# The opening of a two-layer hybrid encoder: forget-gate products in column groups, token blocks turned while the rows of x arrive

## The reference

```python
proj = x @ w_in                       # 1024 x (3*1024 + 16)
q, k, v, fg = jnp.split(proj, [D_MODEL, 2 * D_MODEL, 3 * D_MODEL], axis=-1)
log_f = jax.nn.log_sigmoid((fg + b_f).astype(jnp.float32))
c = jnp.cumsum(log_f, axis=1).transpose(0, 2, 1)
...
logits = jnp.einsum("bhqd,bhkd->bhqk", q_i, k).astype(jnp.float32) * scale
logits = logits + c_i[..., None] - c[:, :, None, :]
mask = pos_k[None, :] <= pos_q[:, None]
probs = jax.nn.softmax(jnp.where(mask, logits, -jnp.inf), axis=-1)
...
x = layer_norm(ALPHA * x + m, ln1_g[i], ln1_b[i])
```

## Time and profile before

| what | us |
|---|---|
| median of 3 runs | 1293.03 |
| lowest and highest | 1290.93, 1293.05 |
| the profiled execution's own time | 1291.16 |
| its span | 1289.4 |
| PE busy | 1262.9 (98%) |
| POOL busy | 862.1 (67%) |
| DVE busy | 538.6 (42%) |
| ACT busy | 408.1 (32%) |

### The profile page before, as it was taken

The page is one execution under the profiler, slowest core; times in us unless marked ns, Lnnn a source line. Parts: engine busy times, 40 slices in busy tenths (PEclk is TensorE's granted clock), DMA queues, the critical chain, the costliest instruction groups (busy, mean ns, idle before and its releaser), DMA issues.

```text
span 1289.4 us, 17594 instructions
## 1 busy us (share of the span) xinstructions
PE 1262.9 (98%) x5758; PEld 1014.5 (79%) x5758; DVE 538.6 (42%) x826; ACT 408.1 (32%) x678; POOL 862.1 (67%) x1166
## 2 busy tenths in 40 slices
PE   7999999989999999999999999989999999999998
PEld 3777777768888888888888767868888888888886
DVE  6544454473444444301254365273434444301252
ACT  1544444313333333300044385113333333300041
POOL 6445555547878787777477556747878787777573
PEclk9999999989999999999999999989999999999999
DMA  5111122212322223333243222312322224333221
GB/s 189 54 65 64 58 106 82 83 50 82 113 97 89 98 91 130 115 97 98 82 147 114 82 66 82 114 50 85 111 98 90 97 91 130 114 98 98 82 91 57
DMA packets 57146, 120.58 MB, mean 94 GB/s; under 512 B 3744, under 2 KB 35808, under 8 KB 56592
## 3 DMA queue, kind: packets, MB, share of 16 engines
q1 hardware_dynamic: 56048, 117.45, 27.9%
q10 hardware_dynamic: 1056, 2.58, 0.6%
HBM read 117.83 MB, written 2.20 MB: 93 GB/s over the span
## 4 chain that ended last, share of the span: by engine, by line
PE 85%; issue 5%; POOL 3%; POOLq 2%; DVE 2%; ACT 1%; DMA 1%; DVEq 0%; ACTq 0%; SPq 0%
PE bank L409 18%; PE bank L411 18%; PE bank L410 18%; PE bank L430 6%; PE bank L429 6%; PE bank L428 6%; PE bank L663 2%; PE bank L664 2%; PE bank L668 2%; POOLq L392 2%; PE bank L525 1%; PE bank L512 1%; POOL w_lo L395 1%; POOL far_lo L395 1%; POOLq L390 1%
## 5 line engine op out<-in xcount | busy, mean ns | idle before, releaser
L395 POOL TENSOR_TENSOR w_lo<-stage,w_hi 128x256 fp32r<-128x256 f32 x800 | 592.8, 772 | 29.4 <-issue 0.3
L391 POOL TENSOR_SCALAR w_hi<-stage 128x1024 fp32r<-128x1024 f32 x200 | 211.7, 1059 | 170.8 <-PE bank L430 72.9
L409 PE MATMUL bank<-x_hi,w_hi 128*128 128x512 f32 x704 | 274.2, 390 | 0.0
L410 PE MATMUL bank<-x_lo,w_hi 128*128 128x512 f32 x704 | 273.9, 389 | 0.0
L411 PE MATMUL bank<-x_hi,w_lo 128*128 128x512 f32 x704 | 273.9, 389 | 0.0
L389 POOL TENSOR_TENSOR waiter<-waiter 128x1 f32<-128x1 f32 x112 | 24.4, 218 | 203.7 <-PE bank L411 132.4
L411 PEld LDWEIGHTS bank<-x_hi,w_lo 128*128 128x128 f32 x704 | 132.2, 188 | 27.6
L410 PEld LDWEIGHTS bank<-x_lo,w_hi 128*128 128x128 f32 x704 | 132.2, 188 | 27.3
L409 PEld LDWEIGHTS bank<-x_hi,w_hi 128*128 128x128 f32 x704 | 132.2, 188 | 27.2
L1042 DVE SCALAR_TENSOR_TENSOR tmp<-bank,cols,tmp 128x511 f32<-128x511 f32 x88 | 66.0, 750 | 209.7 <-ACT tmp L1296 198.7
L428 PE MATMUL bank<-w_hi,h_hi 128*128 128x512 f32 x352 | 137.3, 390 | 0.0
(11 more groups left out here) (166 smaller groups left out, 1790.7 us busy)
## 6 DMA issues: line engine op xcount, KB each, us to landing
stage<-w_square SPq DMA_DIRECT2D x164, 512.0 KB, 3.3
stage<-w_down SPq DMA_DIRECT2D x44, 512.0 KB, 3.7
rows<-norm_rows SPq DMA_DIRECT2D x4, 1024.0 KB, 5.5
outT<-x SPq DMA_DIRECT2D x8, 256.0 KB, 2.0
x<-xT SPq DMA_DIRECT2D x2, 512.0 KB, 5.0
x<-xT ACTq DMA_DIRECT2D x2, 512.0 KB, 8.4
p_in<-pT ACTq DMA_DIRECT2D x2, 512.0 KB, 3.4
w_ai<-w_lru SPq DMA_DIRECT2D x1, 1024.0 KB, 8.1
```

The lines of the kernel that those rows point to most:

```text
L391: pool.tensor_scalar(high[:, s, :], stage[:, s, :], 1.0, 0.0, ALU.mult, ALU.add)
L395: piece = pool.tensor_tensor(low[:, s, to], stage[:, s, to], high[:, s, to].bitcast(F32), ALU.subtract)
L409: pe.matmul(out, w_hi[:, s, c:c + P], m_hi, start=first, stop=False)
L410: pe.matmul(out, w_hi[:, s, c:c + P], m_lo, start=False, stop=False)
```

## The change

1. **Loads.** SP takes x tiles 0 to 3 and 6, 7, and holds the other units back until tiles 6, 7 have landed; ACT's queue takes the forget weights, then unit 0, then x tiles 4, 5, then the bias and the column constants.
2. **Forget products.** The weights arrive in `wf_in`; DVE copies them into `wf`, now 32 wide per k-tile with zeros behind the 16 columns. Product k writes partitions 32(k mod 4) to 32(k mod 4)+31 of bank 5, so four partial sums stand in four column groups of the array. `turn_forget` multiplies `z_chan` by `pick` (ones where a head's four partial sums stand), which turns and adds them in one product.
3. **Order on PE.** Products and blocks 0 to 4 come as x tiles arrive; then the 8 hi x hi products of unit 0, which wait only for its high half (`first_high`), `turn_forget`, the 8 lo x hi, blocks 5 and 6, the 8 hi x lo, block 7; then k; then `sum_forget` and `turn_columns`; then v, into bank 5.
4. **DVE.** The bias is added between the sixth and the seventh `in_lo`; the log1p keeps its square, read by seven steps, in bank 6 (PSUM) and no longer in SBUF.
5. **ACT.** All eight blocks and the casts of k come before the store of `c_rows`; before, three of the blocks did, and the casts waited behind the store.
6. **Slots.** The first iteration of `qkv`, `up0` and `up1` is written out on SP and POOL, with wait counts of its own. POOL's waits for PE become weaker there: for the four units of `up0` the count `unit_used` goes from 33, 34, 35, 36 to 29, 30, 31, 32, and for `up1` likewise from 133.. to 129... A small multiply (L389) falls away in these iterations.

```diff
-    def __init__(self, slots, iters, first, filled, split_lead, used_lead):
+    def __init__(self, slots, iters, first, filled, split_lead, used_lead, split_first, used_first):
...
     def slot_free(self, i, r):
-        return i * len(self.slots) + (self.first + r + 1 + SLOTS - self.used_lead[r])
+        lead = self.used_first if isinstance(i, int) else self.used_lead
+        return i * len(self.slots) + (self.first + r + 1 + SLOTS - lead[r])
...
         def rounds(engine, ph):
-            if ph.iters == 1:
-                yield 0
-            else:
-                with engine.Fori(0, ph.iters) as i:
+            yield 0
+            if ph.iters > 1:
+                with engine.Fori(1, ph.iters) as i:
                     yield i
...
         def _(sp):
-            for n in range(KT // 4):
+            for n in (0, 1, 3):
                 sp.dma_start(x[:, 2 * n:2 * n + 2, :], xT[:, 2 * n:2 * n + 2, :]).then_inc(x_loaded[n], 16)
+            sp.wait_ge(x_loaded[3], 16)
...
-            pe.wait_ge(fg_w_loaded, 32)
-            for k in range(KT):
-                if k % 2 == 0:
-                    pe.wait_ge(x_loaded[k // 2], 16)
-                mm = pe.matmul(banks[5][0:HEADS, :], wf[:, k, :], x[:, k, :], start=(k == 0), stop=(k == KT - 1))
-            mm.then_inc(fg_done, 1)
+            def forget(k):
+                g = k % 4 * QUAD
+                mm = pe.matmul(banks[5][g:g + QUAD, :], wf[:, k, :], x[:, k, :], start=(k < 4), stop=(k >= 4),
+                               skip_group_check=True)
+                if k == KT - 1:
+                    mm.then_inc(fg_done, 1)
...
-            pe.wait_ge(x_lo_ready, KT)
-            project(0, 0, 0, {1: turn_forget})
-            project(0, 1, 1, {3: sum_forget, 4: lambda: first_block(0), 5: lambda: first_block(1),
-                              6: lambda: first_block(2)})
-            pe.wait_ge(q_read, 1)
-            project(0, 2, 0, {1: turn_columns, 2: lambda: first_block(3), 3: lambda: first_block(4),
-                              4: lambda: first_block(5), 5: lambda: first_block(6), 6: lambda: first_block(7)})
+            pe.wait_ge(fg_padded, 2)
+            pe.wait_ge(consts_set, 1)
+            for n in range(KT // 2):
+                pe.wait_ge(x_loaded[n], 16)
+                forget(2 * n)
+                forget(2 * n + 1)
+                for m in {0: (0, 1), 1: (2, 3), 2: (), 3: (4,)}[n]:
+                    first_block(m)
+            pe.wait_ge(first_high, 1)
+            for k in range(KT):
+                pe.wait_ge(x_hi_ready, k + 1)
+                first_pass(w_hi, in_hi, k, first=(k == 0))
+            turn_forget()
+            unit_ready(qkv, 0, 0)
+            for k in range(KT):
+                first_pass(w_lo, in_hi, k)
+            first_block(5)
+            first_block(6)
+            for k in range(KT):
+                pe.wait_ge(x_lo_ready, k + 1)
+                mm = first_pass(w_hi, in_lo, k, last=(k == KT - 1))
+            mm.then_inc(unit_used, 1)
+            first_block(7)
+            pe.wait_ge(x_tok_ready, 5)
+            project(0, 1, 1)
+            sum_forget()
+            turn_columns()
+            project(0, 2, 5)
...
+            dve.wait_ge(fg_w_loaded, 16)
+            dve.tensor_copy(wf[:, :, 0:HEADS], wf_in[:]).then_inc(fg_padded, 1)
...
-            log1p_twice(r0, e, r1, r1, acc)
+            square = banks[6][:, 3 * P:3 * P + QT * HEADS]
+            log1p_twice(r0, e, r1, square, acc)
...
-            act.dma_start(wf[:], w_forget).then_inc(fg_w_loaded, 16)
-            act.dma_start(bf[:], b_forget).then_inc(fg_w_loaded, 16)
-            for n in range(KT // 4, KT // 2):
-                act.dma_start(x[:, 2 * n:2 * n + 2, :], xT[:, 2 * n:2 * n + 2, :]).then_inc(x_loaded[n], 16)
+            act.dma_start(wf_in[:], w_forget).then_inc(fg_w_loaded, 16)
+            act.dma_start(stage[:, 0, :], w_square[0]).then_inc(unit_loaded[0], 16)
+            act.dma_start(x[:, 4:6, :], xT[:, 4:6, :]).then_inc(x_loaded[2], 16)
+            act.wait_ge(fg_padded, 1)
+            act.dma_start(bf[0:HEADS, :], b_forget).then_inc(fg_b_loaded, 16)
             act.dma_start(cols[:], columns).then_inc(cols_loaded, 16)
```

More of the change, by code:

```diff
@@ L120, in plan @@
         last_used[SLOTS:] = [first - 1] * SLOTS
-        split_lead, used_lead = [10 ** 6] * len(slots), [10 ** 6] * len(slots)
+        split_lead, used_lead, split_first, used_first = [], [], [], []
         before, at = list(filled), first
-        for _ in range(iters):
+        for i in range(iters):
             for r, s in enumerate(slots):
-                split_lead[r] = min(split_lead[r], at - last_split[s % SLOTS])
-                used_lead[r] = min(used_lead[r], at - last_used[s])
+                if i < 2:
+                    (split_lead if i else split_first).append(at - last_split[s % SLOTS])
+                    (used_lead if i else used_first).append(at - last_used[s])
+                assert i < 2 or (split_lead[r], used_lead[r]) == (at - last_split[s % SLOTS], at - last_used[s])
                 last_split[s % SLOTS] = last_used[s] = at
@@ L129, in plan @@
                 at += 1
-        phases[name] = Phase(slots, iters, first, before, split_lead, used_lead)
+        phases[name] = Phase(slots, iters, first, before, split_lead, used_lead, split_first, used_first)
         first = at
@@ L386, in _ @@
                         pool.wait_ge(unit_used, ph.slot_free(i, r))
-                        if ph.iters > 1:
+                        if not isinstance(i, int):
                             pool.tensor_tensor(waiter[:], waiter[:], waiter[:], ALU.mult)
                             pool.drain()
-                        pool.tensor_scalar(high[:, s, :], stage[:, s, :], 1.0, 0.0, ALU.mult, ALU.add)
+                        whole = pool.tensor_scalar(high[:, s, :], stage[:, s, :], 1.0, 0.0, ALU.mult, ALU.add)
+                        if ph is phases["qkv"] and isinstance(i, int) and r == 0:
+                            whole.then_inc(first_high, 1)
                         pool.drain()
@@ L1215, in keys @@
                               .rearrange("a s h n -> (a s) h n")).then_inc(row_loaded, 16)
-                for to in (k_a, k_b):
-                    for h in range(2):
-                        act.copy(to[0:HEAD_DIM, h, :], banks[1][h * HEAD_DIM:(h + 1) * HEAD_DIM, :])
-                act.drain()
-                act.sem_inc(kv_read, 1)
+            def keys(j):
+                act.wait_ge(unit_used, phases["qkv"].done(j, 1))
+                act.wait_ge(s_done, j * 2)
+                key_rows(j)
+                key_tiles(j)
             def values(j, turned):
@@ L1225, in values @@
                     act.wait_ge(vt_done, j)
-                act.copy(v_chan[:], banks[VALUE_BANK if turned else 0][:]).then_inc(kv_read, 1)
+                act.copy(v_chan[:], banks[VALUE_BANK if turned else 5][:]).then_inc(kv_read, 1)
             def token_values(j):
@@ L1270, in _ @@
             act.sem_inc(exp_ready, 1)
-            keys(0, False)
-            act.wait_ge(flat_done, 1)
-            act.copy(flat[:].rearrange("p a n -> p (a n)"), banks[6][0:32, P:P + DEPTH * P]).then_inc(flat_read, 1)
-            for m in range(3, KT):
-                token_block(m, 2 + m % 3)
+            key_rows(0)
             act.wait_ge(flat_read, 1)
```

80 lines of the change are left out of this document (57 added, 23 removed).

## The result

The changed kernel takes 1278.49 us (median of 4 runs, 1278.07 to 1280.16), the kernel before 1291.98 in the same comparison; the ratio is 0.9898 with a 95% interval of 0.9885 to 0.991. The forecast was 1283.2 in a range from 1279.5. The direction was right. All runs of this document are fast ones.

A forecast was written before the change was run, and what follows sets the result against it. PE, busy 98% of the span, was taken to bound the kernel, through its waits and low clock before the first scores. Gains 7.6 + 0.4 + 0.8 = 8.8 us from 1291.16 gave 1282.4; forecast 1283.2, range 1279.5 to 1288.

The forecast's parts named there:

- Start: PE's first forget product: would wait for weights and a DVE copy, starting about 5.6 instead of 5.92, 0.3 us gained.
- Forget product: Forget products in column groups: 11 slots of 0.43, 4.7 us at full speed, 2.2 us less; bounds 0 and 3.1.
- my reading of the value sums: Value sums with 64 columns: 10 slots (4.3 us) done in 2.37, factor 0.55, taken as the 3.1 us bound.
- Low clock: PE's opening with five blocks woven in: slow stretch bounded by time, extra kept at 3 us, so 0 gained.
- The rival by which turnings keep the clock low: Opening products broken up by turnings might not raise the clock: gain only 5 to 6 us, 1286.5; chance 0.08.
- The wait of 3.5, the sum, the new turning: Before the scores: PE's wait for DVE's forget row goes, 3.5 us; running sum 1.9 less; new turning costs 0.2.
- The rows: Rows in DRAM (sum, `c_rows`, store, load): scores could start between 36.4 and 38.1 against 37.2; 0.3 us of loss.
- the row path decides: Rival: square in PSUM does not help, DVE reaches `c_rows` at 33.1, gain 8.8 - 2.5, 1285.7; chance 0.13.
- Arrival: Loads of x: tiles 6 and 7 land near 9.5, PE reaches the last pairs at about 12, no wait added.
- Behind the scores: First maxima: DVE's log1p for layer 1 comes 8.8 earlier, so PE's wait for `probs_t` goes, 0.4 us gained.
- up0 and up1: Starts of up0 and up1: POOL may start earlier, so PE's waits for its units go, 0.8 us in all.
- Better overlap and an earlier clock: Rival: forget product saves 3.1, slow stretch 1 to 2 us shorter, gain 10 to 12, 1281; chance 0.12.

The follow-up runs named there:

- warm-up: Changed kernel with eight unread turnings, or one unread fp32 product of 512 columns, ahead of the first forget product: 1278.63 and 1279.04 us.
- the two with the old opening: The kernel before, unaltered, 1291.98 us, and the kernel before with only the first iteration of up0 and up1 written out and POOL's waits weakened, 1289.76 us.

## Why the prediction was wrong

- **Start**: forecast 0.3 earlier, in fact 0.3 later (6.22). The weights landed 5.1 us after their issue, not 4.4, and DVE's copy stands behind them. In the place of the small bias a transfer of 512 KB now follows them on ACT's queue; with the old order of loads, where that holds too, they took 5.2 and 5.1. That this is the cause was not tested.
- **Forget product**: this is the step that failed. "the second instruction of one product cannot overtake the first on the same columns, but the next product can run beside it", hence 11 slots, 4.7 us. The 11 slots come from starting each product beside the second pass of the one ahead. In the trace it starts beside the first, with 0.93, 0.98 and 1.0 us at full speed, 2.9 in all: pairs run two abreast and four products four abreast, at 1.9 and 3.6 times the speed of one group. 4.0 us saved, not 2.2, and more than the 3.1 that the prediction had as its bound. The Trainium skill's rule (up to 4 times for 32 columns, "TensorEngine Tiling (Array Packing)", Theoretical Speedup) was nearer than my reading of the value sums. They mixed four widths and only two groups, and I put my own model of the order of passes above both.
- **Low clock**: forecast 3 us of extra in both; the changed kernel had 1.8 (7.12 us, less 2.9 of products and 2.45 of blocks at full speed). So 1.3 us were saved here where none were forecast. From the first forget product to the first product of q it was 7.05 to 8.18 us in the ten profiles with this opening and no warm-up, so the extra was between 1.7 and 2.8, under 3 in all of them. The rival by which turnings keep the clock low did not come true: the full clock came by the end of the first eight turnings, at 9.93, and came over 3 us later when they were taken out and PE idled for 0.8. The Trainium skill's rule beside it ("TensorE: Matmul & The Clock Gate", Part 4: PE-mode transpose) is neither borne out nor refuted by that, since products ran among the turnings.
- **The wait of 3.5, the sum, the new turning**: 3.5, 1.7 and 0.45 against 3.5, 1.9 and 0.2. Right, the last two a little off: the turning takes 0.81 from start to start, not 0.6.
- **The rows**: PE's wait is 0.75 where it had been idle for 0.41 before, 0.3 lost, as forecast. That path had 2 us of cover from the shorter log1p (DVE waited 2.0 us for the sum). Without the bank the prediction's rival "the row path decides" would have come true, and its price, put at 2.5 us, was 5.1 in that run, since I did not count the low clock behind a wait.
- **Arrival**: PE did not wait for rows of x, though tiles 6 and 7 landed at 10.6, not 9.5, and tiles 4 and 5 at 10.8.
- **Behind the scores**: 0.8 against 0.4. PE was idle for 0.41 there before, and the kernels are 0.55 further apart behind that wait; the other 0.2 is gained by the second scores and not explained.
- **up0 and up1**: 1.5 and 0.3 against 0.8 in all. The waits account for 0.4 to 1.0, a moving clock for about 0.6 at up0, which is luck; 0.4 in the recurrence, where a wait for DVE shrank from 1.3 to 0.9, stays unexplained. It was there in all variants of the changed kernel and in neither of the two with the old opening.

Together at the scores: -0.3, forget and clock 5.3, 3.5, 1.7, -0.45, -0.3 make 9.4, against 7.6. Of the 3.6 us that the forecast fell short, 1.8 are here, and behind the scores come 0.4 for the first pair, 1.0 for up0 and up1 and 0.4 for the recurrence. What came true was the rival "Better overlap and an earlier clock" (0.12), and more of it than its 1281. The range was too narrow below because it treated the overlap as known within 1 us when its two bounds stood 3 us apart. The second set of executions of the changed kernel (1279.16) lies below it as well, though only by 0.3.

## What to carry to other kernels

Products that fill a quarter of the array's columns should be issued in fours into four column groups: here four plain fp32 products took 1.0 us, where one alone takes 0.9 (a quarter of 3.55). Price a wait of PE near 3 us with the slow stretch behind it (here 2.6 us on top of a wait of 3.0), and a DVE chain of small steps with the POOL work beside it. Profile the same kernel twice before a difference under 1.5 us is put down to a change. When one wait is removed from an opening, look at what stands behind it in order on ACT and DVE before moving anything: two of the steps here lost 2 to 3 us at a place that PE had not been waiting for, or hardly.

## What was not expected of the hardware

Both passes of four fp32 products in four column groups had their weights loaded at once and ran four abreast, 1.0 us against 3.55. Twenty turnings woven into an opening did not visibly delay the full clock: slow for 3.5 to 6.0 us with them, 5.5 in the kernel before without. The moment at which the clock rose moved by 0.8 us between two profiles of the changed kernel (second pair 0.98 and 1.22 us from start to start) and was about 2 us later in three profiles of variants that had done the same PE work until then; what sets it was not found. A step of 64 elements per partition took DVE 0.29 us from start to start with one operand in PSUM and 0.62 with both in SBUF, while POOL worked in SBUF in both.
